# Two kinds of work moved in a weight-streaming kernel: small table operations placed earlier, and 32 TensorE transposes given to VectorE

## The reference

```python
# first layer
y_a = gated_deltanet_branch(q, k, v, z, scal, ...)        # ends in @ w_up
y_f = fourier_branch(f, w_fourier)                        # ends in @ w_lin
x = x + (gate_a * y_a + gate_f * y_f) @ w_o
h = rms_norm(x, g_mlp)
x = x + jnp.square(jax.nn.relu(h @ w_mlp_up)) @ w_mlp_down
x = rms_norm(x, g_final)
# second layer
proj = rms_norm_2(x, pre_g) @ w_in
y_a = spatial_gating(a_u, a_v, ...) * jax.nn.silu(a_g)
y_b = s5_branch(b_x, a_re, a_im, log_dt, ...) * jax.nn.silu(b_g)
y_x = memory_cross_attention(x_q, rms_norm_2(mem, mem_g), xa_wk, xa_wv) * jax.nn.silu(x_g)
merged = jnp.sum(gates * branch, axis=2)
out = x + rms_norm_2(merged @ w_out, post_g)
```

## Time and profile before

| | us |
|---|---|
| median of 3 runs | 2400.58 (2400.37 to 2401.02) |
| the profiled execution's own time | 2403.19 |
| its span, first to last instruction | 2401.0 |
| PE busy | 2379.5 |
| DVE busy | 1744.6 |
| ACT busy | 1031.4 |
| POOL busy | 272.6 |

### The profile page before, as it was taken

One profiled execution on the slowest core, in us unless ns is written; L12 is line 12 of the kernel. 1 busy time (PEld: TensorE's weight loads), 2 busy tenths in 40 slices (PEclk: granted clock), 3 DMA queues, 4 the chain that ended last, 5 costly groups with the idle time before them and its releaser, 6 DMA issues.

```text
span 2401.0 us, 29968 instructions
## 1 busy us (share of the span) xinstructions
PE 2379.5 (99%) x12578; PEld 1950.2 (81%) x12578; DVE 1744.6 (73%) x1990; ACT 1031.4 (43%) x857; POOL 272.6 (11%) x226
## 2 busy tenths in 40 slices
PE   8999999999999999999999999999999999999998
PEld 7888788878888888888888888777777788888886
DVE  6465557557697887786766788989999967458865
ACT  5553345334344544444444435443334444544432
POOL 1002201210000000000000000055556400000000
PEclk9999999999999999999999999999999999999999
DMA  7343354347655555555555556565555586566753
GB/s 268 131 167 133 141 184 167 117 156 258 258 193 189 195 194 211 193 193 193 193 193 193 193 211 218 198 237 185 196 193 197 181 298 244 184 232 234 257 196 140
DMA packets 84230, 475.16 MB, mean 198 GB/s; under 512 B 8704, under 2 KB 8832, under 8 KB 32512
## 3 DMA queue, kind: packets, MB, share of 16 engines
q1 hardware_dynamic: 84096, 473.25, 55.5%
HBM read 450.15 MB, written 23.07 MB: 197 GB/s over the span
## 4 chain that ended last, share of the span: by engine, by line
PE 95%; DVE 3%; DMA 1%; issue 0%; ACT 0%; DVEq 0%; SPq 0%; ACTq 0%
PE acc L2161 29%; PE acc L2167 29%; PE acc L2164 29%; PE banks L2306 2%; PE banks L2355 1%; DVE w_lo L1253 1%; PE banks L2422 1%; PE banks L2435 1%; DMA raw<-in_w 1%; PE banks L2178 1%; DMA spilled<-stage 1%; PE banks L2475 0%; PE banks L2457 0%; PE banks L2280 0%; DMA gate_in<-spilled 0%
## 5 line engine op out<-in xcount | busy, mean ns | idle before, releaser
L1253 DVE TENSOR_TENSOR w_lo<-raw,w_hi 128x2048 fp32r<-128x2048 f32 x394 | 908.7, 2308 | 395.3 <-ACT w_hi L794 392.6
L794 ACT ACTIVATE w_hi<-raw 128x2048 fp32r<-128x2048 f32 x394 | 752.8, 1915 | 656.0 <-DMA raw<-in_w 655.8
L2161 PE MATMUL acc<-w_hi,a_hi 128*128 128x512 f32 x2112 | 838.2, 397 | 2.7 <-ACT a_hi L814 1.6
L2164 PE MATMUL acc<-w_lo,a_hi 128*128 128x512 f32 x2112 | 823.8, 390 | 0.0
L2167 PE MATMUL acc<-w_hi,a_lo 128*128 128x512 f32 x2112 | 823.7, 390 | 0.0
L2161 PEld LDWEIGHTS acc<-w_hi,a_hi 128*128 128x128 f32 x2112 | 397.0, 188 | 100.4 <-issue 15.4
L2167 PEld LDWEIGHTS acc<-w_hi,a_lo 128*128 128x128 f32 x2112 | 396.8, 188 | 84.7 <-DVE a_lo L1289 0.3
L2164 PEld LDWEIGHTS acc<-w_lo,a_hi 128*128 128x128 f32 x2112 | 397.4, 188 | 79.1
L2161 PE MATMUL acc<-w_hi,b_hi 128*128 128x512 f32 x928 | 361.7, 390 | 0.0
L2167 PE MATMUL acc<-w_hi,b_lo 128*128 128x512 f32 x928 | 361.1, 389 | 0.0
L2164 PE MATMUL acc<-w_lo,b_hi 128*128 128x512 f32 x928 | 361.0, 389 | 0.0
(11 more groups left out here) (353 smaller groups left out, 1681.3 us busy)
## 6 DMA issues: line engine op xcount, KB each, us to landing
raw<-in_w SPq DMA_DIRECT2D x395, 1024.0 KB, 4.8
spilled<-stage SPq DMA_DIRECT2D x72, 256.0 KB, 5.9
gate_in<-spilled SPq DMA_DIRECT2D x20, 512.0 KB, 5.8
x_rows<-in_x SPq DMA_DIRECT2D x4, 512.0 KB, 8.4
x_rows<-in_x SPq DMA_DIRECT2D x1, 2048.0 KB, 9.4
mem_rows<-in_mem SPq DMA_DIRECT2D x2, 1024.0 KB, 5.8
spilled<-stage_b SPq DMA_DIRECT2D x8, 256.0 KB, 5.9
out<-y_rows SPq DMA_DIRECT2D x3, 512.0 KB, 2.7
```

The lines of the kernel that those rows point to most:

```text
L794: act.activation(w_hi[:, n % HIGH, :], raw[:, n % RAW, :], ACT.Copy)\
L1253: dve.tensor_tensor(w_lo[:, n % RAW, :], raw[:, n % RAW, :], w_hi[:, n % HIGH, :].bitcast(F32), ALU.subtract).then_inc(lo_split, 1)
L2161: pe.matmul(o, hi[:, tk], wh, start=first, stop=False)
L2164: pe.matmul(o, hi[:, tk], wl, start=False, stop=False)
```

## The change

- `ssm_small` part 0 goes from slot 242 to slot 234, part 1 from slot 244 to slot 237, so 8 and 7 slots sooner.
- Quarter 0 of the two inputs isn't turned by TensorE any more. VectorE turns it with 16 transposes of 32 x 256 blocks (`turn_first`), in six parts at places 166 to 171 for `w_o` and 750 to 755 for `w_out`. ScalarE makes the high half (`first_hi`, places 172 and 756), VectorE the low half (`first_lo`, places 174 and 758).
- The keys aren't turned by TensorE any more. VectorE turns `km_rows` straight into `kmT` with 16 transposes of 32 x 512 in eight parts at places 665 to 672. ScalarE's four copies go. `load_vm` stays at its place and waits for VectorE's last part.

```diff
-        put_at(2 * end("w_dn_up", n) + 2, "y_in", n)
+        if n:
+            put_at(2 * end("w_dn_up", n) + 2, "y_in", n)
...
-        put_at(2 * end("w_branch1", n) + 2, "merge_in", n)
+        if n:
+            put_at(2 * end("w_branch1", n) + 2, "merge_in", n)
...
+    for tag, name in (("y", "w_dn_up"), ("merge", "w_branch1")):
+        at = 2 * end(name, 0) + 2
+        for part in range(6):
+            put_at(at + part, "turn_first", tag, part)
+        put_at(at + 6, "first_hi", tag)
+        put_at(at + 8, "first_lo", tag)
...
-    put(end("xa_wv", 1) + 2, "ssm_small", 0)
-    put(end("xa_wv", 1) + 4, "ssm_small", 1)
+    put(end("xa_wv", 0) - 2, "ssm_small", 0)
+    put(end("xa_wv", 0) + 1, "ssm_small", 1)
...
     for part in range(8):
         put_at(2 * a + 17 + part, "turn_plain", "sg", part)
+        put_at(2 * a + 25 + part, "turn_plain", "km", part)
...
-    put(a, "xa_k")
...
             def load_mem(t):
                 if t == 0:
                     sp.wait_ge(pe_done, me.at("y.T"))
+                    sp.wait_ge(dve_done, me.at("y.first.T"))
...
             def load_vm():
-                sp.wait_ge(pe_done, me.at("km.T"))
+                sp.wait_ge(dve_done, me.at("km.T"))
                 load_rows(vm, "xa_wv", loaded["vm"])
...
+            def first_hi(tag):
+                act.wait_ge(dve_done, me.at(f"{tag}.first.T"))
+                for t in range(NT):
+                    at = (slice(None), slice(0, 4), slice(t * P, (t + 1) * P))
+                    act.activation(b_hi[0][at], b_raw[0][at], ACT.Copy).then_inc(act_done, me.done(f"{tag}.{t}.hi"))
...
+            def turn_first(tag, part):
+                name = {"y": "w_fourier", "merge": "w_branch0"}[tag]
+                if part == 0:
+                    dve.wait_ge(pe_used, end(name, 3))
+                    dve.wait_ge(dve_done, me.at("w_dn_up0.y" if tag == "y" else "w_branch10.y"))
+                turn_strips(y_rows[:, :, 0:NW], b_raw[0][:, 0:4, :], 3 * part, min(3, 16 - 3 * part), (f"{tag}.first.T",))
+
+            def first_lo(tag):
+                for t in range(NT):
+                    at = (slice(None), slice(0, 4), slice(t * P, (t + 1) * P))
+                    dve.wait_ge(act_done, me.at(f"{tag}.{t}.hi"))
+                    dve.tensor_tensor(b_lo[0][at], b_raw[0][at], b_hi[0][at].bitcast(F32), ALU.subtract)\
+                        .then_inc(dve_done, me.done(f"{tag}.{t}.lo"))
...
             def xa_score(h):
-                pe.wait_ge(act_done, me.at("km.3.t", "xq.3.t"))
+                pe.wait_ge(dve_done, me.at("km.T"))
+                pe.wait_ge(act_done, me.at("xq.3.t"))
```

More of the change, by code:

```diff
@@ L574, in build @@
                  "xo": (a_raw[:, 0:KW, :], a_hi[:, 0:KW, :], a_lo[:, 0:KW, :]),
+                 "km": (kmT[:, :, :],),
                  "glu": (a_raw[:, KW:, :], a_hi[:, KW:, :], a_lo[:, KW:, :])}
@@ L1043, in turned @@
             def turned(tag, dst, scale):
-                if tag == "km":
-                    act.wait_ge(dve_done, me.at("sg.T"))
                 for j in range(4):
@@ L1090, in _ @@
                      "sg_norm": lambda part: root("sgn", 64, NT) if part == 0 else None,
-                     "gelu_turn": gelu_turn, "plain_hi": plain_hi,
-                     "xa_k": lambda: turned("km", kmT, 1.0), "xa_q": lambda: turned("xq", xqT, 1.0 / 16),
+                     "gelu_turn": gelu_turn, "plain_hi": plain_hi, "first_hi": first_hi,
+                     "xa_q": lambda: turned("xq", xqT, 1.0 / 16),
                      "xa_score": xa_score, "xa_prob": xa_prob, "xa_out": xa_out,
@@ L2001, in turn_plain @@
                         dve.wait_ge(pe_used, end("w2_gate2", 3))
-                    dve.wait_ge(dve_done, me.at({"sg": "sg.gated", "xo": "xo.rows", "glu": "glu.rows"}[tag]))
+                    if tag == "km":
+                        dve.wait_ge(loaded["km"], 32)
+                        dve.wait_ge(dve_done, me.at("sg.T"))
+                    else:
+                        dve.wait_ge(dve_done, me.at({"sg": "sg.gated", "xo": "xo.rows", "glu": "glu.rows"}[tag]))
                 for o in range(2 * part, 2 * part + 2):
@@ L2010, in turn_plain @@
                     else:
-                        src = (av if tag == "sg" else glu)[at, :, :].rearrange("p t (k d i) -> p d t k i", d=4, i=32)[:, d]
+                        src = {"sg": av, "km": km_rows, "glu": glu}[tag][at, :, :].rearrange("p t (k d i) -> p d t k i", d=4, i=32)[:, d]
                         dst = raw_rows[to].rearrange("p k (t c) -> p t k c", t=NT)[:, :, :, at]
@@ L2059, in _ @@
                      "ssm_small": ssm_small, "ssm": ssm, "sg_norm": sg_norm, "sg_mix": sg_mix,
-                     "gelu_turn": gelu_turn, "xa_score": xa_score, "turn_plain": turn_plain, "plain_lo": plain_lo,
+                     "gelu_turn": gelu_turn, "xa_score": xa_score, "turn_plain": turn_plain, "turn_first": turn_first, "first_lo": first_lo, "plain_lo": plain_lo,
                      "xa_gate": xa_gate, "glu_rest": glu_rest, "glu_gate": glu_gate}
@@ L2485, in glu_rest @@
                     ins.then_inc(pe_done, me.done(f"gr.{j}.T", "gelu_rows.T"))
-            def xa_k():
-                pe.wait_ge(loaded["km"], 32)
-                turned("km", lambda t, k: km_rows[:, t, k * P:(k + 1) * P])
             def xa_q():
@@ L2500, in _ @@
                      "ssm_u": ssm_u, "ssm": ssm, "sg_mix": sg_mix,
-                     "xa_k": xa_k, "xa_q": xa_q, "xa_score": xa_score, "xa_prob": xa_prob,
+                     "xa_q": xa_q, "xa_score": xa_score, "xa_prob": xa_prob,
                      "xa_out": xa_out, "glu_rest": glu_rest,
```

## The result

The changed kernel takes 2412.42 us (median of 5 runs, 2411.48 to 2413.46), the kernel before 2400.58 (5 runs, 2400.32 to 2401.52): a ratio of 1.0046, 95% interval 1.0034 to 1.0057, so +11.8 us. The same two kernels on another chip gave 2412.58 and 2402.77, +9.8 us, 1.0039 (1.0025 to 1.0053). The forecast was +6.2 us and slower. The side was right; the first time lies 0.4 us above the upper end of the range (2412) and the rise was 1.9 times the forecast's, on the other chip 1.6 times.

A forecast was written before the change was run, and what follows sets the result against it. TensorE, busy 99% of the span, was taken as the bound. Tables +1.0, quarters +1.3 and keys +3.9 sum to +6.2 us, a median of 2406.8 us; own range 2404 to 2410, wider range 2400 to 2412.

The forecast's parts named there:

- Tables: Units 240 to 251: moved table parts make TensorE wait 3.8 us at unit 240, old waits shrink; net +1.0 us.
- the slow clock once more: Behind the wait at unit 240: TensorE runs at its lower clock again, costing 1.62 us.
- twice 1.62: Upper bound for the slow clock behind the wait at unit 240; the lower bound was nothing.
- 0.8 of rest: Old second wait, 1.28 us in unit 250: a wait of 0.8 us remains ahead of unit 251, bounds 0 and 1.28.
- Quarters: Units 88 and 380: each waits 1.5 us for the low half against 0.90 of transposes saved; +1.3 us together.
- Keys: Unit 338: held SP issues its load late; -1.7 transposes, +3.9 wait, +1.6 slow clock, +3.9 us in all.
- the lower end plus 1.1: Unit 338's load behind the 1 MB of values: ready at 2056.5, between 2055.4 and 2059.6.
- the forecast's 2045.3 for `km.T`: VectorE's last turn of the keys ends at 2045.3; SP then issues the values, and unit 338's load at 2046.3.
- SP's wait is not hidden: Rival at unit 338: SP's wait is hidden, so 3.9 + 1.6 go; +0.7, 2401.3 us; chance 0.15.
- the quarters do wait: Rival at units 88 and 380: they start on time, -1.8 instead of +1.3; 2403.7 us; chance 0.12.
- the lead does not absorb it: Rival: VectorE's additions stay inside the splits' lead everywhere, decided at unit 240; -8.7, 2391.9 us; chance 0.06.
- The dear case: Rival: unit 338's load takes 9.0 us (+3.1), or 1.5 us waits lower the clock (+3.2); 2410 to 2413; chance 0.15.

The follow-up runs named there:

- tables alone: The kernel before with only the two table parts moved, to slots 234 and 237: 2403.98 us against 2401.71 for before, ratio 1.0009.
- quarters sooner: Kernel before with only the first quarters turned by VectorE, in four parts instead of six, high and low halves two places earlier: 2398.74 us, ratio 0.9988.
- SP held: Kernel before, VectorE's work unchanged, with one added wait holding SP ahead of the values until TensorE finished unit 336: 2409.52 us, ratio 1.0033.
- values later: The changed kernel with load_vm moved from slot 334 to 337, behind the loads of units 338 to 340: 2404.21 us, ratio 1.0008 to before.
- the same kernel again: The changed kernel, unaltered, measured once more on another chip: 2412.58 us against 2402.77 for before, ratio 1.0039.
- keys alone: The kernel before with only the keys turned by VectorE, load_vm at its old place waiting for the last turn: 2407.15 us, ratio 1.0021.
- values behind: Changed kernel with SP held at the same step, but the values' two loads moved behind those of units 338 to 340: 2407.38 us, ratio 1.0021 to before.
- quarters alone: The kernel before with only the first quarters of the two operands turned by VectorE, in six parts: 2403.04 us, ratio 1.0004.

## Why the prediction was right, and where its sizes were off

**Tables.** The place and the size of the wait were right: 5.48 us of lead against 9.30 of work gave 3.8, and 4.1 came. The wait was taken from one spot and a longer one laid at another, as written. What was mis-sized is the term behind it: "I charge the slow clock once more, 1.62" and it was 2.5. I had given twice 1.62 as the bound and took the value of the 2.2 us wait for a 3.9 us one. Against it, 0.4 came back at unit 250, where I had 0.8 of rest and 0.4 was left. Net +1.8 for +1.0, and 2.0 in the profile of tables alone.

**Quarters.** Right in each step: `first_hi` starts at 625.04, the split of unit 88 at 626.09 behind it, `b_lo` of the third quarter at 630.24 and `first_lo` at 631.43. VectorE's and ScalarE's timelines:

```profile
630.24 1.28 DVE L1282 TENSOR_TENSOR b_lo<-banks,b_hi 128x512 fp32r<-128x512 f32 x2
631.43 1.28 DVE L2022 TENSOR_TENSOR b_lo<-b_raw,b_hi 128x512 fp32r<-128x512 f32 x2
```

```profile
625.04 1.15 ACT L918 ACTIVATE b_hi<-b_raw 128x512 fp32r<-128x512 f32 x2 [5.73 <-DVE b_raw L1314]
626.09 1.90 ACT L804 ACTIVATE w_hi<-raw 128x2048 fp32r<-128x2048 f32 x1
```

That ends at 632.71, and TensorE starts unit 88 at 632.82. The price was 1.66 and 1.62 of wait where 1.5 stood, and 0.12 in the unit behind, no slow clock in either place: +1.7 for +1.3. The kernel with the quarters sooner shows that the order of these steps was the cause.

**Keys.** The mechanism was the forecast's, shown by the held SP alone and by the values moved later. Its size was off in three terms, and this is the most of the miss: +7.1 for +3.9. (1) "I take the lower end plus 1.1": the 1 MB of values cost 2.6, so 7.5 us from issue to split where I had 5.9. The Trainium skill, "DMA: Bandwidth & Descriptors", section "Anatomy of one DMA", gave an estimate of 2.4 for it by bytes over its rate, from a fit to DMAs that GpSimd issues; SP issues those here, and the 2.6 agrees within 0.2. I ought to have gone nearer to it than to nothing. (2) SP came free 1.1 us later than worked out. Unit 337 started at 2047.50, 1.9 after the place that 2047.31 less the 1.67 of the transposes gives; the forecast's 2045.3 for `km.T`, moved by these 1.9, is 2047.2, and it ended at 2048.35. The load of unit 332 had taken 7.85 us to its split where it took 6.70 before, and held VectorE's chain with it; as shown above, this differs between executions, so it is not a term that the rows of one profile could give. Nor were the leads of the splits of 335 to 337 the 3 us that I wrote: they were 2.4, 1.8 and 2.1, which was enough. (3) The clock behind the long wait cost 2.2 and not 1.62. Terms (1) and (2) make 6.6 of wait from 3.9.

**The clock.** A stretch at 1.2 GHz came with each of the two long waits, as forecast, but it lasted 6.83 us, from 1465.35 and from 2059.27, and not 3.41 as from 1504.32 in before. That ends with TensorE at work again, as the Trainium skill, "TensorE: Matmul & The Clock Gate", section "Part 1: The HAM clock gate", has it: the throttled clock is the default, activity lifts it. Two units of the same work, the first behind the same 3.9 us wait, in tables alone and with the values later:

```profile
1465.14:1473.56 8.42, 8.42 (x24) 6.65 (x25) 8.14 (x12) 2.73 (x3) 0.00 (x0) 0.64 0.29 109
```

```profile
1466.90:1474.11 7.21, 7.21 (x24) 5.72 (x25) 6.93 (x12) 1.53 (x3) 0.00 (x0) 0.76 0.31 114
```

The two lengths can be told apart by when the clock fell. In the changed kernel it fell 1.45 and 1.86 us before TensorE went on (the same kernel again: 1.20 and 1.50), with tables alone 0.75, with keys alone 1.75 and with SP held 3.0 before: 6.83 us each. In before it fell with TensorE's restart (1504.32 against 1504.36), with the values later 1.37 and with the values behind 1.37 after it: 3.41 us each. The part of the stretch in which TensorE worked, at half speed, is what is paid: half of 6.83 - 1.45 is 2.7 where unit 240 lost 2.5, half of 3.41 is 1.7 where unit 247 of before lost 1.6. The wait at unit 240 was the same 3.9 us in the tables-alone kernel and in the last two of these, so the length of the wait alone doesn't decide. What sets the moment of the fall stays open; no run was made for it.

**The rivals.** SP's wait is not hidden (6.3 us), the quarters do wait, and the lead does not absorb it. The dear case came: its term, the load in 9.0 us, was half right (7.5), its other, a slow clock behind the 1.5 us waits, didn't come at all. I had given it 0.15 and an upper end of 2412 us that leaves half of it out. That the measured 2412.42 lies within the 2410 to 2413 of this rival is luck: the sum got there by SP's later release and by longer slow stretches behind the long waits, of which the rival has neither. The account of the profile is +10.7; the medians' +11.8 (interval +8.2 to +13.7) and +9.8 lie on either side of it, and the runs don't tell the three apart. The range should have reached to the 7.0 us of wait that I had myself worked out as the bound, and to twice the clock.

## What to carry to other kernels

A step that is moved from TensorE to a less busy engine also moves the moment at which others are released. Look first for a semaphore wait in the queue that issues loads: here it held SP for 18.3 us, which came back as a wait of 6.3 us on TensorE and 2.2 us for a slow clock, and moving the waiting step behind three prefetches was worth more than the whole change had at stake in that place. Work given to a full engine has to be cut into pieces smaller than the smallest lead that it passes (9.3 us behind a lead of 5.5 lost 4; in three pieces at later places, each with a split in between, it lost nothing in two profiles and 0.5 us in a third). No run has the pieces without the other places, so how much each of the two gave isn't shown. Where two costs of the nearest rows lie far apart, the wider end belongs in the range.

## What the runs showed that was not expected

- What could be won at the tables was itself no fixed number. Unit 246 lasted 7.92 us in before, and with the tables at the same places 6.57 in quarters alone, 7.00 in keys alone, 7.90 in quarters sooner and 8.55 with SP held. The load of unit 244 had taken 7.07, 5.71, 6.18, 7.03 and 7.69 us to land, and in the kernel before the chain that ends in the wait begins with that load. In all five the unit lasts 0.82 to 0.87 us longer than the load took. In the two short cases no slow clock followed, so that units 246, 247 and 250 together cost some 3 us in one profile and 5.9 in another, where the forecast took 5.2 from the only one that it had:

```profile
1498.27:1504.84 6.57, 5.75 (x26) 4.34 (x24) 5.99 (x20) 3.55 (x2) 0.00 (x0) 1.00 0.45 163
1504.84:1510.84 6.00, 5.85 (x25) 4.47 (x25) 5.96 (x7) 0.39 (x2) 0.00 (x0) 1.00 0.47 175
```

- The same 3.9 us wait of TensorE ahead of unit 240 was followed by 6.83 us at the lower clock in three profiles (2.5 to 2.9 us lost; the changed kernel, the same again, tables alone) and by 3.41 us in two (1.6 to 1.7 lost). Neither the 1.5 us waits nor the 2.0 us wait of the kernel with the values behind were followed by any, though the 2.2 us wait of before was. A price for a wait of 3.9 us is therefore a range and not a number, from 1.6 to 2.9 us.
- A load of 1 MB right behind another 1 MB, after SP had issued nothing for 18 us, took 7.5 us from issue to use, 4.9 with nothing ahead: 2.6 us more.
- VectorE's lateness and SP's add: a load that is late by 1.2 us early in the stretch (unit 332) moved the turns, the turns moved SP, and SP moved the load of unit 338. This is why keys alone waited 1.5 us less at unit 338 than the changed kernel (5.15 against 6.64): the two differ in what that load took, 6.7 and 7.9 us. That the other parts of the change had a hand in it isn't shown.
